# A one-core block of two models: a wait moved in the last stage, squares in PSUM, activation tables loaded at other places

## What is computed

```python
def sq_relu_mlp(h, w_up, w_down):                 # plain feed-forward, hidden width 4096, twice
    return jnp.square(jax.nn.relu(h @ w_up)) @ w_down
def swiglu(x, w_gate, w_up, w_down):              # gated feed-forward, hidden width 2816, twice
    return (jax.nn.silu(x @ w_gate) * (x @ w_up)) @ w_down
uv = jax.nn.gelu(h @ w_in)                        # start of gMLP; u, v = split(uv)
...
h = h + rms_norm(m, g[1])                         # each branch of the first block is normed and added
f = sq_relu_mlp(rms_norm(h, g[2]), w_up[layer], w_down[layer])
h = h + rms_norm(f, g[3])
...
gate = jax.nn.sigmoid(rms_norm_2(h, ple_norm[i]) @ w_ple_gate[i])   # last stage
h = h + gate * (p[i] @ w_ple_proj[i])
return rms_norm_2(h, final_norm)
```

## Time and profile before

| | |
|---|---|
| three timed runs | 2481.40, 2481.31, 2479.49 us; median 2481.31 us |
| profiled execution | 2479.67 us, span 2477.9 us |
| mean granted clock of TensorE | 0.984 of 2.4 GHz |
| busy: TensorE / VectorE / ScalarE / GpSimd | 2399.2 (97%) / 1112.5 (45%) / 563.3 (23%) / 1739.4 (70%) us |
| matmuls | 11070 |

### The profile page before, as it was taken

How to read it: one execution, slowest core, us unless ns; L and a number is a source line. 1 busy time by engine, 2 the same in 40 slices (tenths; PEclk the granted TensorE clock), 3 DMA queues, 4 the chain that set the end, 5 groups by cost and what they waited for, 6 DMA issues and landing times.

```text
span 2477.9 us, 31448 instructions
## 1 busy us (share of the span) xinstructions
PE 2399.2 (97%) x11070; PEld 1941.6 (78%) x11070; DVE 1112.5 (45%) x1584; ACT 563.3 (23%) x1039; POOL 1739.4 (70%) x827
## 2 busy tenths in 40 slices
PE   8999999999999999999999999998999999999998
PEld 6777888877777788887888888676678888888876
DVE  3445323454444532447424335478573334342345
ACT  2322101132553210113201013321621121010031
POOL 8657877776445787785888887565248887888765
PEclk9999999999999999999999999999999999999999
DMA  5222333323222233332233323232112333333322
GB/s 180 85 68 85 102 93 100 95 85 100 84 68 69 77 102 95 94 104 77 86 109 93 100 85 100 64 102 68 31 51 89 102 102 94 94 96 99 89 73 77
DMA packets 64665, 221.08 MB, mean 89 GB/s; under 512 B 7360, under 2 KB 9664, under 8 KB 64448
## 3 DMA queue, kind: packets, MB, share of 16 engines
q1 hardware_dynamic: 60336, 210.27, 28.4%
q10 hardware_dynamic: 4240, 9.57, 1.3%
HBM read 217.71 MB, written 2.10 MB: 89 GB/s over the span
## 4 chain that ended last, share of the span: by engine, by line
PE 89%; DVE 6%; ACT 2%; issue 2%; DMA 0%; DVEq 0%; POOL 0%; ACTq 0%; SPq 0%; POOLq 0%
PE PS L366 21%; PE PS L360 21%; PE PS L361 21%; PE PS L437 4%; PE PS L371 4%; PE PS L373 4%; PE PS L372 4%; PE PS L413 1%; PE PS L414 1%; PE PS L417 1%; PE PS L637 1%; DVE MK L1572 1%; PE PS L658 1%; PE PS L647 1%; DVE TOP L1571 1%
## 5 line engine op out<-in xcount | busy, mean ns | idle before, releaser
L326 POOL TENSOR_TENSOR WH<-RAW,ONES 128x1024 fp32r<-128x1024 f32 (+3 forms) x411 | 767.1, 1866 | 682.0 <-PE PS L366 270.8
L329 POOL TENSOR_TENSOR WL<-RAW,WH 128x1024 fp32r<-128x1024 f32 (+3 forms) x411 | 976.8, 2377 | 32.2
L360 PE MATMUL PS<-XH,WH 128*128 128x512 f32 x1568 | 615.9, 393 | 9.8 <-DVE PTL L1698 5.4
L361 PE MATMUL PS<-XL,WH 128*128 128x512 f32 x1568 | 613.2, 391 | 0.0
L366 PE MATMUL PS<-XH,WL 128*128 128x512 f32 x1568 | 387.9, 389 | 0.0
L360 PEld LDWEIGHTS PS<-XH,WH 128*128 128x128 f32 x1568 | 296.4, 189 | 80.1 <-issue 10.9
L361 PEld LDWEIGHTS PS<-XL,WH 128*128 128x128 f32 x1568 | 296.3, 189 | 61.0
L366 PEld LDWEIGHTS PS<-XH,WL 128*128 128x128 f32 x1568 | 294.0, 188 | 62.8 <-issue 1.6
L1312 DVE TENSOR_TENSOR HL<-T,HH 128x512 f32 x108 | 233.5, 2162 | 152.1 <-ACT HH L945 107.7
L360 PE MATMUL PS<-HH,WH 128*128 128x512 f32 x712 | 277.2, 389 | 2.0 <-DVE HL L1632 2.0
L361 PE MATMUL PS<-HL,WH 128*128 128x512 f32 x712 | 277.0, 389 | 0.0
(11 more groups left out here) (232 smaller groups left out, 2941.4 us busy)
## 6 DMA issues: line engine op xcount, KB each, us to landing
RAW<-in_weights SPq DMA_DIRECT2D x379, 512.0 KB, 3.5
RAW<-in_weights SPq DMA_DIRECT2D x16, 384.0 KB, 3.1
H<-in_xT SPq DMA_DIRECT2D x8, 256.0 KB, 6.4
BIAS<-in_rel ACTq DMA_DIRECT2D x8, 256.0 KB, 3.4
RAW<-in_weights SPq DMA_DIRECT2D x8, 256.0 KB, 2.7
out<-R ACTq DMA_DIRECT2D x8, 256.0 KB, 2.2
BIAS<-in_rel ACTq DMA_DIRECT2D x8, 224.0 KB, 3.8
DECAY<-in_decay ACTq DMA_DIRECT2D x1, 1024.0 KB, 4.7
```

Of the source, the lines that this page charges most:

```text
L326: nc.gpsimd.tensor_tensor(WH[:, slot, 0:w], raw, ONES[:, 0:1].to_broadcast([P, w]), ALU.mult).then_inc(high_split, 1)
L329: nc.gpsimd.tensor_tensor(WL[:, slot, 0:w], raw, WH[:, slot, 0:w].bitcast(F32), ALU.subtract).then_inc(weights_split, 1)
L360: nc.tensor.matmul(PS[:, slot, :], WH[:, slot, w], xh[:, k, :], start=(k == 0), stop=False)
L361: nc.tensor.matmul(PS[:, slot, :], WH[:, slot, w], xl[:, k, :], start=False, stop=False)
```

## The change

It has three parts. (1) The wait for PTH and PTL moves from in front of `first_products` into it, behind the first unit and `stat_sum`; in the calls whose units all have the same number of tiles nothing is waited for. (2) In the plain feed-forward the square goes to PSUM bank 5 and not to T[1]; ScalarE's copy to HH and VectorE's subtraction read it there. (3) `table_of` runs a function on four columns of ONES into a scratch tile, so that the compiler puts the table load there: for Gelu right behind the first root, for the root between the seventh and the eighth square of each branch, and in the last stage between the last sigmoid and the last square.

```diff
+        SCRATCH = at("SCRATCH", 204.4375, [P, 4])
...
                 product(tiles, xh, xl, xr)
                 stat_sum()
+                if tiles != others[0][0]:
+                    pe.wait_ge(h_ready, hr.next(others[0][0]))
                 for n, (tiles, xh, xl) in enumerate(others):
...
-            pe.wait_ge(h_ready, hr.next(2))
             first_products((DT, XH, XL), (2, PTH, PTL), (DT, XH, XL), (2, PTH, PTL))
...
+            def table_of(function):
+
+                S.activation(SCRATCH[:], ONES[:, 0:4], function)
...
                     square(m[:, t, :])
+                    if t == DT - 2:
+                        table_of(ACT.Sqrt)
...
-                            S.activation(T[:, 1, :], T[:, 0, :], ACT.Square).then_inc(act_self, 1)
+                            S.activation(PS[:, 5, :], T[:, 0, :], ACT.Square).then_inc(act_self, 1)
                             act.wait_ge(act_self, me.next())
                             passed()
-                            S.activation(HH[:, bass.ds(i * 4 + s, 1), :], T[:, 1:2, :], ACT.Copy)\
+                            S.activation(HH[:, bass.ds(i * 4 + s, 1), :], PS[:, 5:6, :], ACT.Copy)\
...
             stat()
+            table_of(ACT.Gelu_apprx_tanh)
             act.wait_ge(ri_ready, 1)
...
                 ev.next()
+                if t == DT - 1:
+                    table_of(ACT.Sqrt)
                 act.wait_ge(residual, hn.next())
                 square(H[:, t, :])
...
-                    V.tensor_tensor(HL[:, f, :], T[:, src:src + 1, :], HH[:, f, :].bitcast(F32),
+                    V.tensor_tensor(HL[:, f, :], src, HH[:, f, :].bitcast(F32),
...
-                            low(i, 4, s, 1)
+                            low(i, 4, s, PS[:, 5:6, :])
...
-                            low(i, 2, s, 2)
+                            low(i, 2, s, T[:, 2:3, :])
```

## The result

The changed kernel takes 2464.17 us in the median of four runs (2462.64 to 2465.96), against 2480.4 for the kernel before in the same session (2478.69 to 2481.4): ratio 0.9936, 95% interval 0.9924 to 0.9948, or 13 to 19 us less. Forecast were 2465.7 us in a range of 2461 to 2473. Run again beside later experiments it took 2465.52 us (2464.57 to 2466.07), ratio 0.9948 [0.9934, 0.9961].

What follows compares the result with a forecast made beforehand. TensorE's waits and half-clock stretches were taken as the bound. Terms 2.9 + 0.5 + 4.5 + 6.9 = 14.8 us off 2479.67 gave 2464.9, plus 0.8 for run levels: 2465.7 us, range 2461 to 2473.

Steps and rivals of the forecast that it cites:

- Gelu table: First gelu: loading its table before ScalarE's wait shortens TensorE's gap and keeps the clock up; 2.9 us, bounds 1.3 and 2.9.
- The 1.3 us of load: First gelu: the evacuation starts as the matmuls end, without the table load between; 1.3 us saved.
- The 1.6 us of clock: Behind the first gelu gap: eight matmuls run at full instead of half clock; 1.6 us.
- Root tables: Branch norms: fetching the root's table ahead saves 0.17 us at three places; 0.5 us, bounds -0.3 to 0.7.
- A drain behind the load: Each table load adds a 1.38 us drain, so the last square comes late; 2467.2 us for that rival, chance 0.02.
- Squares in PSUM: Start of both plain feed-forwards: GpSimd's six splits end sooner, TensorE waits less; 4.5 us, bounds 0 and 6.0.
- Collision: Rival, plain feed-forward: GpSimd and VectorE still collide as HH stays in SBUF; 4.5 us lost, 2470.2 us, chance 0.09.
- bank 5: Rival, plain feed-forward: accesses to PSUM bank 5 hold up matmuls; 2504 us at 0.2 us each, chance 0.02.
- The instruction-long lock: Plain feed-forward: two-SBUF-input VectorE and GpSimd operations exclude each other for whole instructions; 6.0 us instead of 4.5.
- Last stage: Last stage: the first unit runs beside the wait for PTL and the clock stays up; 6.9 us, bounds 4.5 and 6.9.
- a lower bound that gives the clock 2.4: Last stage: if the clock falls for twelve matmuls, 2.4 us go and 4.5 us remain.
- The eighth tile: Last stage: the first unit's eighth XL tile is late next, ending at 2401.31 us; ten matmuls follow it.

Runs made afterwards that it cites:

- a profile without the tables: Kernel before with the moved last-stage wait and the squares in PSUM, no table load moved; 2467.56 us, ratio 0.9957.
- the tables alone: Kernel before with only the gelu and root table loads moved ahead; 2478.25 us, ratio 1.0004.
- the time of the part alone: Kernel before with only the plain feed-forward's squares moved to PSUM; 2473.85 us, ratio 0.9983.
- the one put back: Changed kernel plus one unread VectorE subtraction with two SBUF inputs per plain hidden tile; 2468.97 us, ratio 0.9965.
- that of the part alone: Kernel before with only the last stage's wait moved behind the first unit; 2472.23 us, ratio 0.997.
- the fill: Kernel before with 24 unread matmuls ahead of the last stage's wait for PTL; 2477.91 us, ratio 0.9999.

## Why the prediction was right

- **Bound.** TensorE's gaps and slow stretches were the right ledger: in the two profiles compared, the four terms account for 14.9 of the 17.0 us. That they come so near the forecast term by term has luck in it, as the clock parts of two of them are not there in every run.
- **Gelu table**, forecast 2.9: 2.86 in the excess of that place (4.21 to 1.35), gap 0.93 us, no half clock behind it. The 1.3 us of load are shown, also against a profile without the tables. The 1.6 us of clock were luck in part: of the six profiles with the 2.21 us wait only three have half clock behind it, and the one that the sum was made against was one of them. My reason for the clock was wrong as well: I concluded from a wait of 2.69 us that a shorter one is safe, and the tables alone showed that wait with half clock behind it. Behind the 0.93 us wait the clock was full in all eight profiles that have it, which is some support but no proof for every run.
- **Root tables**, forecast 0.5: 3 x 0.17 as read. A drain behind the load, which the Trainium skill gives ("ScalarE: Activation LUTs", What ACT_TABLE_LOAD costs), does not show: 35.01 - 33.72 - 1.28 = 0.01 us, and in the last stage load and dummy take 1.50 of the hole of 1.56.
- **Squares in PSUM**, forecast 4.5: 4.75 in the two places (2.38 + 2.37), 4.9 in the time of the part alone. The six splits took 26.06 us where 26.04 were forecast. Collision and bank 5 fall by the same run. The 2.162 us that I gave the old subtraction were a mean over both kinds of tile (plain ones 2.48); no term of the sum hung on it. The instruction-long lock of the Trainium skill ("SBUF — State Buffer", Who interferes with whom) would have emptied the wait; 0.74 us stayed, and the split loses 0.33 us a unit to it (4.67 against 4.34) and 0.27 to the one put back (4.61); it is VectorE's own operation that gives way most, with 1.86 us for the one put back instead of 0.69.
- **Last stage**, forecast 6.9: 6.74 up to the sums, in both profiles of the changed kernel and in that of the part alone. Inside the term I had 5.2 for the start and 1.7 for the clock, beside a lower bound that gives the clock 2.4; the fill shows 2.3, so the bound was the better figure. The eighth tile is late next, as worked out. That the clock stays up held for the first unit and not behind it: in five of eight profiles half clock in the second unit takes 1.6 us back, and the whole is then worth 5.2.
- **The sum** missed 2.2 us of the profiled run. The range had one more half-clock stretch in it for that, on the low side. It is chance by the run more than effect of the change: the second profile of the same kernel has a span 1.9 us longer, 15.1 us less than before, and there the half clock of the last stage and of the restart at 1845 us is back.
- **Parts against whole.** By medians the parts alone give 6.5, 4.9 and 0.5 us (11.9) and the whole 13.1 to 16.2. The tables' worth at the end is open, and so is how much of the difference is the clock's scatter.

## What to carry to other kernels

Price a change at the few places where the bounding engine waits, and ask there which engine it waits for: 91 us less of VectorE work gave nothing, and 23 us at the right place 4.9. A short wait of TensorE costs its length and, sometimes, a half-clock stretch behind it; take that second part as a chance, not as a yes or no read from one profile (the gelu wait: three of six), and measure such terms with many rounds. Where a wait can't be shortened, matmuls that nobody reads can hold the clock up, provided that they end before the awaited operand is there; look also at the next unit, where half clock can come instead.

## What was not expected of the hardware

- The same kernel and the same gap (2.43 us between starts, up to the one at 1845 us) had 1.00 behind it in one profile and 0.51 in another; the wait of 2.7 us at 221 us and that of 2.2 us at the gelu likewise, in programs that are the same up to there. A local gain of 3 us upstream can so vanish at the end.
- 24 matmuls that do nothing useful, in a wait of 5.4 us, cost no time and spared the next unit 2.3 us of half clock; 1.6 us of it came back one unit later.
- A releaser in the list of waits may be a coincidence: the name changed from the split to a VectorE operation, while the lag of TensorE behind the split's end stayed 0.20 to 0.21 us in all fourteen profiles; read the lags, not only the name.
